# Expert stage: the products with a tile's upper part come first, the rest after, and two vector operations change places

## The reference

```python
top_vals, top_idx = lax.top_k(t @ router_w + router_b, 2)      # 256 tokens, 8 experts
for e in range(8):
    y = (silu(t @ w_gate[e]) * (t @ w_up[e])) @ w_down[e]      # 1024 -> 3584 -> 1024
    out = out + gates[:, e:e + 1] * y
```

## Time and profile before

| what | value |
|---|---|
| median of 3 runs (lowest to highest) | 2834.48 us (2831.26 to 2835.78) |
| the profiled execution | 2831.9 us |
| its span, first to last instruction | 2830.0 us |
| mean granted clock of TensorE | 0.976 of full speed |
| busy: TensorE | 2662.6 us, 94% |
| busy: VectorE | 2019.2 us, 71% |
| busy: ScalarE | 1474.6 us, 52% |
| expert stage in the span | about 1756 to 2812 us |

### The profile page before, as it was taken

The page is one execution under the profiler, slowest core; times in us unless marked ns, Lnnn a source line. Parts: engine busy times, 40 slices in busy tenths (PEclk is TensorE's granted clock), DMA queues, the critical chain, the costliest instruction groups (busy, mean ns, idle before and its releaser), DMA issues.

```text
span 2830.0 us, 46494 instructions
## 1 busy us (share of the span) xinstructions
PE 2662.6 (94%) x18228; PEld 2268.8 (80%) x18228; DVE 2019.2 (71%) x1887; ACT 1474.6 (52%) x1435; POOL 86.3 (3%) x82
## 2 busy tenths in 40 slices
PE   8999989999999889986999897999999999998997
PEld 7888887888888778885889886777777778786875
DVE  6665776666666757656667745888888888887786
ACT  4444514454443514443446623666766666665665
POOL 6000005000000000000000000000000000000000
PEclk9999999999999999998999998999999999999999
DMA  8564213556563206553655402999999999997995
GB/s 274 192 199 135 96 48 128 184 178 193 189 190 119 82 17 193 192 171 99 193 184 149 135 2 79 331 345 340 337 335 339 344 333 338 347 342 270 341 342 201
DMA packets 343042, 601.75 MB, mean 213 GB/s; under 512 B 12000, under 2 KB 180832, under 8 KB 342752
## 3 DMA queue, kind: packets, MB, share of 16 engines
q1 hardware_dynamic: 335264, 590.84, 61.4%
q10 hardware_dynamic: 7616, 8.58, 1.0%
HBM read 598.34 MB, written 1.05 MB: 212 GB/s over the span
## 4 chain that ended last, share of the span: by engine, by line
DMA 54%; PE 22%; DVE 12%; ACT 8%; DVEq 2%; issue 1%; another core or an unknown queue 0%; SPq 0%; ACTq 0%; PEldq 0%; PEld 0%; POOLq 0%
DMA raw<-in_moe_w_up 26%; DMA raw<-in_ffn_w_down 20%; DVE wlo L297 8%; ACT whi L294 6%; PE ps L930 5%; DMA raw<-in_dn_w_in 3%; DMA raw<-in_w_in 2%; PE ps L814 2%; PE ps L553 1%; DVEq L299 1%; DMA raw<-in_pool_w_in 1%; DMA raw<-in_ffn_w_up 1%; PE ps L1298 1%; PE ps L1285 1%; PE ps L1294 1%
## 5 line engine op out<-in xcount | busy, mean ns | idle before, releaser
L297 DVE TENSOR_TENSOR wlo<-raw,whi 128x2048 fp32r<-128x2048 f32 x562 | 1287.2, 2290 | 289.5 <-ACT whi L294 280.4
L294 ACT CAST whi<-raw 128x2048 fp32r<-128x2048 f32 x562 | 1072.4, 1909 | 475.2 <-DMA raw<-in_moe_w_up 150.6
L2637 PE MATMUL ps<-whi,xboth 128*128 128x512 f32 x1792 | 589.8, 400 | 11.8 <-remote 6.3
L529 PE MATMUL ps<-xboth,whi 128*128 128x512 f32 x1680 | 420.7, 392 | 0.0
L2637 PEld LDWEIGHTS ps<-whi,xboth 128*128 128x128 f32 x1792 | 338.3, 189 | 89.9 <-issue 21.4
L529 PEld LDWEIGHTS ps<-xboth,whi 128*128 128x128 f32 x1680 | 305.3, 189 | 57.2
L2637 PE MATMUL ps<-wlo,xboth 128*128 128x512 f32 x896 | 350.7, 391 | 0.0
L532 PEld LDWEIGHTS ps<-xboth,wlo 128*128 128x128 f32 x1680 | 229.2, 190 | 16.4
L532 PE MATMUL ps<-xboth,wlo 128*128 128x256 f32 x1680 | 234.2, 282 | 0.0
L2662 PE MATMUL ps<-whi,hhi 128*128 128x512 f32 x448 | 182.0, 406 | 19.5 <-DVE wlo L297 16.9
L2637 PEld LDWEIGHTS ps<-wlo,xboth 128*128 128x128 f32 x896 | 169.6, 189 | 35.8 <-issue 3.8
(11 more groups left out here) (504 smaller groups left out, 3298.9 us busy)
## 6 DMA issues: line engine op xcount, KB each, us to landing
raw<-in_moe_w_gate SPq DMA_DIRECT2D x112, 1024.0 KB, 5.2
raw<-in_moe_w_up SPq DMA_DIRECT2D x112, 1024.0 KB, 5.4
raw<-in_moe_w_down SPq DMA_DIRECT2D x112, 1024.0 KB, 5.0
raw<-in_ffn_w_gate SPq DMA_DIRECT2D x55, 1024.0 KB, 5.4
raw<-in_ffn_w_up SPq DMA_DIRECT2D x55, 1024.0 KB, 5.4
raw<-in_ffn_w_down SPq DMA_DIRECT2D x55, 1024.0 KB, 4.9
raw<-in_w_in SPq DMA_DIRECT2D x24, 1024.0 KB, 5.3
raw<-in_dn_w_in SPq DMA_DIRECT2D x16, 1024.0 KB, 6.0
```

The costliest lines, as they stand in the source:

```text
L294: act.copy(whi[:, n % SPLIT, 0:width], raw[:, n % RAW, 0:width]).then_inc(hi_ready[n % SPLIT], 1)
L297: dve.tensor_tensor(wlo[:, n % SPLIT, 0:width], raw[:, n % RAW, 0:width], whi[:, n % SPLIT, 0:width], ALU.subtract).then_inc(split_ready[n ...
L529: pe.matmul(ps[:, first_bank + b, :], whi[:, n % SPLIT, c * GW + b * P:c * GW + (b + 1) * P], xboth[:, c].rearrange("p a t -> p (a t)"), s ...
L2637: mm = pe.matmul(dst, (xhi, xlo)[part][:, k * C // 2 + c, xhalf(q)], w[:, (m + k) % SPLIT, c * EW:(c + 1) * EW], start=(k == 0 and c == 0 ...
```

## The change

The change adds three semaphores `hi_seen`, one for each `whi` buffer. In the expert stage ScalarE raises one behind a drain after each upper part. TensorE waits for it at the start of a tile and does the eight matmuls with `whi`, then waits for `split_ready` and does the four with `wlo`. The first three tiles of the stage are split outside of it, so they are waited for as before. In `downs` the two output banks take turns from matmul to matmul in both parts. `gated` gets a hook, through which ScalarE copies the turned sums between Silu and the split of m + 4, and VectorE makes their remainder before that of m + 4 instead of after it.

```diff
--- before.py
+++ after.py
@@ -228,6 +228,7 @@
         tile_done = [sem(f"tile_done{i}") for i in range(SPLIT)]
         hid_ready = [sem(f"hid_ready{i}") for i in range(2)]
         hid_made = sem("hid_made")
+        hi_seen = [sem(f"hi_seen{i}") for i in range(SPLIT)]
         gate_summed = sem("gate_summed")
         gate_copied = sem("gate_copied")
         up_copied = sem("up_copied")
@@ -2629,15 +2630,23 @@
 
         def moe_tensor(pe, n, l):
 
+            watched = n + SPLIT
+
             def by_token(m, dst, q):
                 for k in range(2):
-                    take_split(pe, m + k)
+                    if m + k >= watched:
+                        take(pe, hi_seen[(m + k) % SPLIT])
+                    else:
+                        take_split(pe, m + k)
                     for c in range(C // 2):
-                        for s, (w, part) in enumerate(PASSES):
-                            mm = pe.matmul(dst, (xhi, xlo)[part][:, k * C // 2 + c, xhalf(q)],
-                                           w[:, (m + k) % SPLIT, c * EW:(c + 1) * EW],
-                                           start=(k == 0 and c == 0 and s == 0),
-                                           stop=(k == 1 and c == C // 2 - 1 and s == 2))
+                        for s, xt in enumerate((xhi, xlo)):
+                            pe.matmul(dst, xt[:, k * C // 2 + c, xhalf(q)], whi[:, (m + k) % SPLIT, c * EW:(c + 1) * EW],
+                                      start=(k == 0 and c == 0 and s == 0), stop=False)
+                    if m + k >= watched:
+                        take_split(pe, m + k)
+                    for c in range(C // 2):
+                        mm = pe.matmul(dst, xhi[:, k * C // 2 + c, xhalf(q)], wlo[:, (m + k) % SPLIT, c * EW:(c + 1) * EW],
+                                       start=False, stop=(k == 1 and c == C // 2 - 1))
                     mm.then_inc(tile_done[(m + k) % SPLIT], 1)
 
             def gate(m, g, q):
@@ -2655,14 +2664,19 @@
             def downs(m, g, final=False):
                 take(pe, hid_ready[0])
                 for k in range(2):
+                    take(pe, hi_seen[(m + k) % SPLIT])
+                    for b in range(2):
+                        for h in (hh, hl):
+                            for s in range(2):
+                                pe.matmul(ps[:, s, :], h[:, g % 2, 2 * k + b, :],
+                                          whi[:, (m + k) % SPLIT, b * D + s * HALF:b * D + (s + 1) * HALF],
+                                          start=False, stop=False, skip_group_check=True)
                     take_split(pe, m + k)
                     for b in range(2):
                         for s in range(2):
-                            for p, (w, part) in enumerate(PASSES):
-                                mm = pe.matmul(ps[:, s, :], (hh, hl)[part][:, g % 2, 2 * k + b, :],
-                                               w[:, (m + k) % SPLIT, b * D + s * HALF:b * D + (s + 1) * HALF],
-                                               start=False, stop=(final and k == 1 and b == 1 and p == 2),
-                                               skip_group_check=True)
+                            mm = pe.matmul(ps[:, s, :], hh[:, g % 2, 2 * k + b, :],
+                                           wlo[:, (m + k) % SPLIT, b * D + s * HALF:b * D + (s + 1) * HALF],
+                                           start=False, stop=(final and k == 1 and b == 1), skip_group_check=True)
                     mm.then_inc(tile_done[(m + k) % SPLIT], 1)
                 if final:
                     pe.drain().then_inc(f["y_made"], 1)
@@ -2747,13 +2761,18 @@
             def next_split(m, end):
                 take(act, tile_done[m % SPLIT])
                 if m + SPLIT < end:
-                    split_hi(act, m + SPLIT)
-
-            def gated(m, g, end):
+                    split_seen(m + SPLIT)
+
+            def split_seen(m):
+                split_hi(act, m)
+                act.drain().then_inc(hi_seen[m % SPLIT], 1)
+
+            def gated(m, g, end, between=lambda: None):
                 next_split(m, end)
                 take(act, tile_done[(m + 1) % SPLIT])
                 act.activation(sil[:, g % 2, :], ps[:, 4, :], ACT.Silu)
-                split_hi(act, m + 1 + SPLIT)
+                between()
+                split_seen(m + 1 + SPLIT)
 
             def turned(g):
                 take(act, hid_turned)
@@ -2769,11 +2788,10 @@
             def item(m, q, end, last=False):
                 for g in range(1, EN):
                     G = q * EN + g
-                    gated(m, G, end)
+                    gated(m, G, end, lambda: turned(G - 1))
                     if g == 4:
                         take(act, f["pick_turned"])
                         act.copy(gpick_t, ps[:, 5, 0:2 * P])
-                    turned(G - 1)
                     if g == 5 and not last:
                         take(act, f["gathered"])
                         gather_hi(7, 0, 1 - q).then_inc(f["gather_hi"], 1)
@@ -2852,8 +2869,8 @@
                     elif g == 3:
                         take(dve, f["back"])
                         add_back(3, 1, 1).then_inc(f["bank_read"], 1)
+                    turned(G - 1)
                     refill(m + 1, end)
-                    turned(G - 1)
                     if g == 2:
                         add_back(5, 0, 1)
                     elif g == 5 and not last:
```

## The result

| | before | after |
|---|---|---|
| median of four runs (lowest to highest) | 2833.76 us (2831.26 to 2835.78) | 2802.64 us (2800.49 to 2804.29) |
| the profiled execution, its span | 2831.9, 2830.0 us | 2804.29, 2802.4 us |

The ratio is 0.989 (95% interval 0.9873 to 0.9907): 31.1 us less, where 27.4 were forecast. One execution of a later run (upper parts first, alone) took 6803 us; nothing on record explains it, and that run's ratio leaves it out.

The account below looks back on a forecast made before the run. TensorE was taken as the bound, nearly full except for a regular wait before the down tiles. 25.4 + 2.0 = 27.4 us off a median of 2834.5 gave 2807 us; range 2800 to 2825, the forecast's own 2800 to 2814.

Parts of the forecast that it names:

- The reading of the chain: Chain and wait table point to the up matrix's loads; the prediction held loads ahead and TensorE setting the pace.
- The hole and its cause: Between up and down tiles TensorE loses 0.43 us plus 0.11, awaiting the turned sums' remainder; 47 x 0.54 = 25.4 off.
- Upper parts first gives nothing in the steady state alone: Gate and up tiles may start 1.8 us ahead of their remainder; none waits in steady state, so only slack.
- ScalarE's move: ScalarE copies the turned sums straight after Silu; their remainder then ends 3.0 us before it is wanted.
- The stalls at the exit: At the loop's exit VectorE and ScalarE idle 6.5 and 4.6 us; upper parts first saves 2.0, bounds 0 and 5.6.
- a rival of mine for the worse: Longer instruction lists: ScalarE's loop grows by 84 drains a round, more stalls give back 18.4 us, 2825; chance 0.04.
- Costs set at nothing: Added TensorE waits, added ScalarE drains, VectorE's order, bank order and loads, each taken to cost 0.
- the waits on TensorE: Mid-tile, 333 added waits: cost 0, at most 37 us; rival that they break the stream, 2844, chance 0.07.
- ScalarE's drains: Six added a group, at most 14.7 us an item; hidden under TensorE, cost 0.
- the order of banks: In `downs` the bank changes at each matmul instead of each third; cost 0.
- the loads: Stream must rise from 338 to 347 GB/s; cost 0. Rival that loads become the bound, 2834, chance 0.07.
- VectorE as the next to be late: VectorE at 119.3 us an item against 126.6; rival that it becomes the bound, losing 12.4 us, 2819, chance 0.08.

Follow-up runs that it names:

- the first two experiments: Kernel before with only the two moves (ScalarE's copy, VectorE's remainder of the sums, both earlier): 2815.32 us; changed kernel with both moves undone: 2829.2 us.
- the version without TensorE's drain: Changed kernel with ScalarE's copy of the turned sums in its old place and no TensorE drain behind the first seven items' last down tiles: 2792.67 us.
- the repeat: The changed kernel itself, unedited, run once more on the chip of three other runs: 2803.53 us, ratio 0.9901.
- the run with VectorE's move alone: Changed kernel, upper parts first included, with only ScalarE's copy of the turned sums back behind the first down tile's split: 2797.77 us, ratio 0.9879.
- one pair of these: Changed kernel with VectorE's remainder of the sums back behind the down tile's, so upper parts first plus ScalarE's earlier copy: 2857.77 us, ratio 1.0094.

## Why the prediction was right

**The reading of the chain** held. ScalarE's loads were put down as the bound by the chain and were not; the table after still has 146 us for them (150.6 before) with nothing lost. One row was misread on the way: the twelfth matmul of the first gate tile is the first of the pair at 2221.78, not the second (from 2222.01 there are twelve starts to the last one of the second tile at 2224.50). It ends at 2222.18 as modelled, and ScalarE starts 0.20 behind it; the conclusion stands.

**The hole and its cause**, 47 x 0.54 = 25.4 us: shown. The item of 126.6 us is what the prediction gave (126.5). Group by group the steady gain is 26.8 us: 0.42 in each of 47 up tiles, some 0.15 in the down tiles behind them. The two halves of its argument were taken apart: without the moves the hole stays, without upper parts first a smaller one comes back in the down tiles. That the cause is the sums' remainder, and not the weights' that the profile names, is settled by the first two experiments as a pair.

**Upper parts first gives nothing in the steady state alone**: shown (2829.2). What the prediction missed is that, with the moves made, it is worth another 12 us in all (2815.32 with the moves alone, 2802.64 and 2803.53 with it too): it called it slack, and this slack pays for the later remainders.

**ScalarE's move** was taken as part of what lifts the wait. It is not needed: with the copy in its old place the remainder of the sums still ends 1.6 us before the down tiles start (2126.67 against 2128.28 in one group of that run).

**The stalls at the exit**, 2.0 us with bounds 0 and 5.6: the mis-sized term. It measured 6.4, over its own upper bound. Alone, the moves gave 1.6 of it and upper parts first 3.0, by the same stretch. The two stalls lengthened TensorE's tiles by 6.9 and 7.0 us before and by 4.5 and 3.4 after (another 0.4 is in a later tile). The bound counted earlier tiles and one spell of slow clock; it did not price the second stall, which is in the earlier trace rows as the longest of the 47 waits, 5.0 us, nor its move to another group. How much of its 3.6 us is the move and how much the earlier tiles, no run separates. That the lists' length moves a stall was only a rival of mine for the worse; in the runs its sign is open: 6 us less with one more drain, and no such gain in the version without TensorE's drain.

**The end of the stage and the loop's start** had no term. Here are the windows around the last down tiles (same columns as above), first before and then after the change; the clock fell only in the second:

```profile
2808.00:2815.00 7.00, 5.75 (x24) 4.43 (x24) 0.00 (x0) 1.05 (x2) 0.00 (x0) 1.00 0.03 4
```

```profile
2779.00:2787.00 8.00, 7.18 (x24) 5.40 (x24) 0.00 (x0) 0.65 (x1) 0.00 (x0) 0.79 0.00 0
```

The idle time of TensorE ahead of them is alike, 2.6 us in both; after the change part of the 24 matmuls ran at 1.2 GHz (from 2779.49 on, two starts take 0.85 us instead of 0.46), and they took 1.6 us longer. At the two later starts of the loop, the down tiles and the gate tiles together take 0.5 and 0.8 us longer than before, 1.3 in all; the last item loses 1.8, of which 1.6 are these matmuls. Both work against the forecast, and the two larger gains outweigh them: -26.8 - 6.4 + 1.3 + 1.8 = -30.1, against -30.2 from the stage's third group to its end in the two traces. So the nearness of 27.4 to the measured 31.1 is in part luck: the holes gave 1.4 more than forecast and the stalls 4.4 more, and 3.1 us of costs without a term took back half of that. Ahead of the stage the profiled execution after the change was 2.8 us slower (first gate matmul at 1762.6 against 1759.8); the repeat has it at 1757.8, so this is the spread of executions.

**Costs set at nothing**: the waits on TensorE (nothing in the stream; at one start of the loop the run with 1008 more lost 4.6 us), ScalarE's drains, the order of banks (a down tile of 12 matmuls takes 2.72 us) and the loads are all borne out. The Trainium skill's limit of about 358 GB/s for one core ("DMA: Bandwidth & Descriptors", Specifications) was not reached as a mean, 350, and no tile was late. It did not hold for shorter stretches: slices of 15 us between 1900 and 2500 us ran at up to 388 GB/s, and the burst of the earlier trace rows at 394. VectorE as the next to be late is seen once: in the last item, whose groups have no gathering, the last transposes wait for its product, 0.3 us in the change and longer in the run with VectorE's move alone, whose row is:

```profile
2769.57 0.65 PE L2661 MATMUL ps<-con,work 128*128 128x128 f32 x4 [1.32 <-DVE work L2841]
```

## What to carry to other kernels

Where an engine waits for two things, look at the instruction that stands between the named releaser and the waiter's start: here the 0.69 us behind the blamed one was the cause, and one swap of two lines on VectorE with upper parts first gave all of the steady gain. Test edits of a bundle singly and in pairs: one pair of these made the kernel 0.9% slower, and another edit was worth next to nothing by itself. A drain that only tells what a later semaphore tells anyway can go.

## What the runs showed of the hardware that was not expected

- At the exit from the loop into straight code, VectorE stands still once for 4.6 to 6.8 us and ScalarE once for 2.5 to 8.0, in all twelve profiles; in three of them the view puts ScalarE's down to another engine or a load. The view of the DMA queues has rows for instructions (packets, MB, share). First the change between 2100 and 2540 us, inside the loop, where the second queue has none, then its stall on ScalarE, 2601.9 to 2607.0:

```profile
q8 instruction: 19, 0.31, 0.3%
```

```profile
q14 instruction: 1, 0.01, 0.4%
```

  In each of the 24 stalls one packet of instructions on q14 starts 1.6 to 2.0 us before the stall ends (in this one at 2605.3). So I put these stalls down to the fetching of instructions; it rests on this coincidence and on the drains that moved them. Why the transfer starts only 3.4 us into this stall is not seen. A packet alone makes no stall: with three drains q14 has eight between 2100 and 2500 us, and outside the loop's start the groups there are as long as the change's. Where a stall falls depends on the length and order of the lists: one drain more behind each split moved ScalarE's, and two more moved it to another group. The Trainium skill's small instruction store ("Advanced Engine Details and Errata", ISA Cache) fits this; it gives lines of 16 KB, and the page of the change has 2.00 MB in 122 packets on q8, 16 KB each, but 0.34 MB in 41 on q14, 8 KB each.
- With 1008 more waits TensorE stands idle near the start of two rounds, 2.7 and 2.9 us, and the eight matmuls behind the second start 0.42 apart, at half pace. A packet on q8 starts within each of the two idle spells (2032.8 and 2289.8). The same queue tells the change's loss of 1.0 and 1.3 us there: its packet starts 3.0 and 3.1 us behind the round's first gate matmul, and the gate tiles take 6.57 and 6.84 us. In the run with VectorE's move alone, whose list for TensorE is the same, it is 1.3 and 1.5 us, and they take 5.59 and 5.57; before, 2.5 and 2.6 us, and 5.88 and 5.73. Why the transfer starts later with the same list stays open.
- A drain on TensorE behind 24 matmuls costs 0.42 us: at the end of an item inside a round, the four last down matmuls start at 2154.80 and the next gate tile at 2156.13, 1.33 behind them, of which 0.91 are theirs. The slow start behind it costs 0.13 more (the gate tiles take 5.58 us, and 5.45 without the drain). With the loop's branch the 0.42 are 1.03.
